# First block of sorted tokens: by matmuls with place matrices, where it was scattered, loaded back and transposed

## The chip, the cores and the metric

One Trainium2 chip, one of its cores. TensorE (PE) multiplies, VectorE (DVE), ScalarE (ACT) and GpSimd (POOL) compute elementwise, SyncE (SP) issues most transfers. The metric is the time of one execution on the device in microseconds, the median over runs.

## The reference, cut to what matters

The network is one diffusion block followed by a second block that ends in a mixture of experts. Only that last part is touched. With 512 tokens of 1024 features it computes

```python
group_p, group_idx = lax.top_k(jax.nn.softmax(group_logits, axis=-1), 1)     # 1 of 4 groups
exp_p, exp_idx = lax.top_k(jax.nn.softmax(in_group, axis=-1), 2)             # 2 of its 4 experts
h = silu(einsum("td,edf->tef", t, w_gate)) * einsum("td,edf->tef", t, w_up)  # 16 experts, 256 wide
y = einsum("tef,efd->td", h * combine[:, :, None], w_down)
out = layer_norm(ALPHA * t + y, ln2_g, ln2_b)
```

where t itself is a layer norm of the rows that come before (`(x - mean) * rs * g + b`), and `combine` holds the gates of the two chosen experts.

## The kernel before, in words

All engines run hand-written instruction streams that meet at semaphores. Two stages matter.

**Rows and routing (`OutRows`, `Grouping`).** The last dense product leaves the rows before their layer norm in `X`, token-major, four tiles of 128 tokens. DVE takes the logits, picks each token's group and experts, and counts (with a few small PE matmuls, `pe_count`) which place each token gets when tokens are sorted by group. Places 0 to 127 are block 0, the first 128 tokens of group 0; there are `NBLK` = 7 blocks of 128 places. The place of each token is in `D1` (float) and `dest` (integer). The layer norm is made in two passes per tile into `tok`: `dve_rows_first` (subtract the mean, times the gain; line 2939) and `dve_rows_second` (times the reciprocal deviation, plus the bias; line 2946). After each second pass POOL scatters that tile's rows by `dest` to an array `xs` in device memory (line 3017).

**Experts (`moe`).** 28 steps x, four experts for each block b. A step takes three weight slots of 1 MB, called A and B (the up product) and D (down), in the order A0 B0 A1 B1 D0 A2 B2 D1 and so on, 84 in all. SP loads slot s into one of six raw buffers (line 3206) once DVE is done with slot s-6. ACT makes its high part (`hi`, line 3312), DVE the low part (`lo`, line 3376), and PE multiplies three times (high-high, low-high, high-low; lines 3259 to 3261 and 3285 to 3287). Between the products PE turns the hidden rows (`turn_hidden`, line 3269) after DVE's `gate` (line 3393), and ACT and DVE split them again (lines 3333, 3398). The tokens of a block are loaded back from `xs` into `XB` (block 0 at line 3188), turned by eight PE transposes into banks 6 and 7 (`turn_block`, line 3243), and split by ACT (`x_hi`, line 3319) and DVE (`x_lo`, line 3382) into `xsh` and `xsl`. After its last step DVE evacuates and normalises a block (lines 3408 to 3433), and POOL delivers it (line 3224).

Before block 0 starts, SP, ACT (for slot 5) and DVE wait for all four scatters (`scattered`). DVE's order is then: `lo` of slots 0, 1, 2, `x_lo(0)`, `lo` of slots 3, 4, 5, `gate(0)`, `lo` of slot 6, `hidden_lo(0)`. ACT makes the high parts of slots 0 to 3 early; that of slot 4 overwrites `X` and that of slot 5 overwrites `tok`.

Of the kernel before, what the change touches and what calls it, by code (L numbers as in the profile page):

```python
# [8 lines left out]
ALU = mybir.AluOpType  # L9
# [3 lines left out]
P = 128  # L13
D = 1024
KT = D // P
# [8 lines left out]
NCH = T // P  # L24
# [11 lines left out]
RING_RAW, RING_W = 6, 6  # L36
# [8 lines left out]
TMP = CONST + 4608  # L45
MAIN = TMP + 5 * W * 4 + 1024
# [2668 lines left out]
class OutRows:  # L2715
# [218 lines left out]
    def dve_rows_first(self, dve, tok, ts):  # L2934

        nc = self.e.nc
        dve.wait_ge(self.ln_in, 16)
        for t in ts:
            nc.vector.scalar_tensor_tensor(tok[:, t, 0:D], self.X[:, t, :], self.mv[:, t, 0:1], self.LN1[:, 0:D],
                                           ALU.subtract, ALU.mult).then_inc(self.half_row, 1)  # L2940

    def dve_rows_second(self, dve, tok):

        for t in range(NCH):
            dve.wait_ge(self.half_row, t + 1)
            self.e.nc.vector.scalar_tensor_tensor(tok[:, t, 0:D], tok[:, t, 0:D], self.rs[:, t:t + 1],
                                                  self.LN1[:, D:2 * D], ALU.mult, ALU.add).then_inc(self.row_ready, 1)


class Grouping:  # L2950


    def __init__(self, e, late, tok, dest, gsel):
        self.e, self.st, self.late = e, Stage(e, "route"), late
        self.tok, self.dest, self.gsel = tok, dest, gsel
        off = [TMP + 4096]

        def small(n, *dims):
            t = self.st.sb(n, [P] + list(dims), off[0])
            off[0] += (int(np.prod(dims)) * 4 + 31) // 32 * 32  # L2960
            return t

        self.PRI, self.BASE0 = small("pri", 4), small("base0", 4)
        self.LG, self.EX, self.M1, self.EQ, self.MG, self.IN, self.TM, self.MA, self.MB, self.M2, self.ED, self.SM, \
            self.GP, self.W1, self.W2, self.CI = (small(n, NCH, c) for n, c in (
                ("lg", 32), ("ex", 4), ("m1", 1), ("eq", 4), ("mg", 4), ("in", 4), ("tm", 4), ("ma", 4), ("mb", 4),
                ("m2", 1), ("ed", 1), ("sm", 1), ("gp", 1), ("w1", 1), ("w2", 1), ("ci", 4)))
        self.TRI = self.st.sb("tri", [P, P], MAIN + 140032)
        self.PM, self.GT, self.IG = small("pm", NCH, 4), small("gt", NCH, 4), small("ig", NCH, 4 * EPG)
        self.D1 = small("d1", NCH, 1)  # L2970
        self.NT, self.X1, self.X2, self.EE, self.EB, self.C0, self.DB = (
            small(n, 1, 4) for n in ("nt", "x1", "x2", "ee", "eb", "c0", "db"))
        self.LE, self.GB = small("le", 3, 3), small("gb", 3, 1)
        assert off[0] <= TMP + 8192
        self.const_in, self.e1_pre, self.e1_ready, self.e2_pre, self.e2_ready, self.mg_ready, self.count_psum, \
            self.dest_ready, self.rec_ready, self.gsel_ready, self.chain = (
                self.st.sem(n) for n in ("const_in", "e1_pre", "e1_ready", "e2_pre", "e2_ready", "mg_ready", "count_psum",
                                         "dest_ready", "rec_ready", "gsel_ready", "chain"))
        self.late_chain = self.st.sem("late_chain")

    def sp(self, sp):
        d = self.e.dram
        sp.dma_start(self.PRI[:, :], d["priority"]).then_inc(self.const_in, 16)
        sp.dma_start(self.BASE0[:, :], d["group_base"]).then_inc(self.const_in, 16)
        sp.dma_start(self.TRI[:, :], d["before"]).then_inc(self.const_in, 16)
        sp.dma_start(self.tok[:, :, D:REC], d["rec_tail"]).then_inc(self.const_in, 16)

    def pe_count(self, pe):

        nc, e = self.e.nc, self.e  # L2990
        pe.wait_ge(self.mg_ready, 1)
        pe.wait_ge(self.const_in, 64)
        mg = self.MG[:, :, :].rearrange("p t g -> p (t g)")
        nc.tensor.matmul(e.bank[4][:, 0:16], self.TRI[:, :], mg, start=True, stop=False)
        for t in range(NCH - 1):
            nc.tensor.matmul(e.bank[4][:, 4 * t + 4:16], e.ones[:, :],
                             self.MG[:, t, :].unsqueeze(1).to_broadcast([P, NCH - 1 - t, 4]),
                             start=False, stop=t == NCH - 2)
        nc.tensor.matmul(e.bank[5][:, 0:16], e.ones[:, :], mg, start=True, stop=True).then_inc(self.count_psum, 1)

    def act_logits(self, act):
        nc = self.e.nc
# [17 lines left out]
    def dve(self, dve):  # L3020
        e, nc = self.e, self.e.nc
        done = [0]
        V = nc.vector
# [27 lines left out]
                V.tensor_tensor(out[:, :, :], EQ[:, :, :], wide(M2[:, :, :]), ALU.is_equal).then_inc(last_sem, 1)  # L3051
                dve.wait_ge(last_sem, 1)

        dve.wait_ge(self.const_in, 64)
        V.tensor_scalar(self.C0[:, 0, :], self.BASE0[:, :], -1.0, 384.0, ALU.mult, ALU.add)
        V.memset(self.EB[:, :, :], 0.0)
        self.late.dve_logits(dve, LG, self.tok)
# [32 lines left out]
        link(V.tensor_tensor(self.PM[:, :, :], self.PM[:, :, :], MG[:, :, :], ALU.mult))  # L3090
        link(V.tensor_reduce(self.D1[:, :, :], self.PM[:, :, :], AX, ALU.add))
        V.tensor_copy(self.dest[:, :], self.D1[:, :, 0]).then_inc(self.dest_ready, 1)

        dve.wait_ge(self.e1_ready, 1)
        link(V.tensor_reduce(GP[:, :, :], EX[:, :, :], AX, ALU.add))
# [26 lines left out]
def moe(e, lead, late):  # L3122
# [6 lines left out]
    nc = e.nc  # L3129
    st = Stage(e, "moe")  # L3130
    I32, U32 = mybir.dt.int32, mybir.dt.uint32
    tok = st.sb("tok", [P, NCH, REC], MAIN + 81920)
# [19 lines left out]
    route = Grouping(e, late, tok, dest, gsel)  # L3152
# [14 lines left out]
    slot = {key: s for s, key in enumerate(order)}  # L3167
# [6 lines left out]
    with block_of(e) as block:  # L3174
# [58 lines left out]
        def _(pe):  # L3233
# [3 lines left out]

            def turn_block(b):
                pe.wait_ge(xb_in[b % 2], 16 * (b // 2) + 16)
                if b:  # L3240
                    pe.wait_ge(xs_ready, b)
                for k in range(KT):
                    last = nc.tensor.transpose(e.bank[6 + k // 4][:, (k % 4) * P:(k % 4 + 1) * P],
                                               XB[b % 2][:, k * P:(k + 1) * P], e.ident[:, :])
                last.then_inc(x_turn, 1)
# [41 lines left out]
                        last = nc.tensor.matmul(out, c, w[:, cc], start=False, stop=j == EPG - 1 and k == 1)  # L3287
                last.then_inc(pe_slot, 1)

            turn_block(0)  # L3290
            for x in range(NSTEP):
                if x % EPG == EPG - 1 and x // EPG + 1 < NBLK:
                    turn_block(x // EPG + 1)
# [10 lines left out]
        def _(act):  # L3304
# [9 lines left out]
            def x_hi(b):  # L3314
                act.wait_ge(x_turn, b + 1)
                if b >= 2:
                    act.wait_ge(pe_slot, slot["B", EPG * (b - 1) - 1] + 1)
                for n in range(2):
                    last = nc.scalar.activation(xsh[b % 2][:, 4 * n:4 * n + 4, :],
                                                e.bank[6 + n][:, :].rearrange("p (k t) -> p k t", t=P), ACT.Copy)  # L3320
                last.then_inc(xh_done, 1)
# [20 lines left out]
            for s in range(4):  # L3342
                hi(s)
                if s == 1:
                    route.act_second(act)
            act.wait_ge(late.row_ready, NCH)
            hi(4)
            x_hi(0)
            act.wait_ge(scattered, 16 * NCH)
            hi(5)  # L3350
            for x in range(NSTEP + 1):
# [17 lines left out]
        def _(dve):  # L3369
# [4 lines left out]
            def lo(s):  # L3374
                dve.wait_ge(hi_done, s + 1)
                nc.vector.tensor_tensor(wl[s % RING_W][:, :], raw[s % RING_RAW][:, :], wh[s % RING_W][:, :].bitcast(F32),  # L3376
                                        ALU.subtract).then_inc(lo_done, 1)

            def x_lo(b):
                dve.wait_ge(xh_done, b + 1)  # L3380
                for n in range(2):
                    last = nc.vector.tensor_tensor(xsl[b % 2][:, 4 * n:4 * n + 4, :],  # L3382
                                                   e.bank[6 + n][:, :].rearrange("p (k t) -> p k t", t=P),
                                                   xsh[b % 2][:, 4 * n:4 * n + 4, :].bitcast(F32), ALU.subtract)
                last.then_inc(xs_ready, 1)
# [48 lines left out]
                                               ).then_inc(y_done, 1)  # L3434

            route.dve_groups(dve)
            dve.wait_ge(scattered, 16 * NCH)
            for n in range(3):
                lo(n)
            x_lo(0)  # L3440
            for n in range(3, RING_W):
                lo(n)
            for x in range(NSTEP + 1):
                if x % EPG == EPG - 1 and x // EPG + 1 < NBLK:
# [63 lines left out]
def layout_inputs(i):  # L3508

    g = {n: np.asarray(v) for n, v in i.items()}  # L3510
    dram = {}
# [4 lines left out]
    xf, q, k, v, o, gt, gf, gm = np.split(w_in, np.cumsum([512, 1024, 1024, 1024, 1024, 16, 1024]), axis=1)  # L3516
# [60 lines left out]
    dram["ln2_rows"] = np.ascontiguousarray(np.broadcast_to(np.concatenate([g["ln2_g_2"][0], g["ln2_b_2"][0]]), (P, 2 * D)))  # L3577
    dram["ln1_rows"] = np.ascontiguousarray(np.broadcast_to(np.concatenate([g["ln1_g_2"][0], g["ln1_b_2"][0]]), (P, 2 * D)))
    dram["group_base"] = np.ascontiguousarray(np.broadcast_to(P * np.arange(4, dtype=np.float32), (P, 4)))
    dram["before"] = np.triu(np.ones((P, P), np.float32), 1)  # L3580
    dram["sgu_ln"] = np.ascontiguousarray(
        np.broadcast_to(np.concatenate([g["sgu_ln_g_2"][0], g["sgu_ln_b_2"][0]]), (P, 2 * D)))
# [19 lines left out]
    s, t = np.meshgrid(np.arange(P), np.arange(P), indexing="ij")  # L3602
# [3 lines left out]
    tok, ch = np.kron(dft(T // 64), dft(64)), dft(P)  # L3606
    tok = tok.reshape(T, T // GRID, GRID)[:, :, 0:FQ].reshape(T, FH)
# [160 lines left out]
```

## Time and profile before

| | us |
|---|---|
| median of 3 runs | 2806.11 (2799.13, 2806.11, 2806.12) |
| the profiled execution, its own time | 2809.66 |
| its span in the trace | 2807.4 |
| mean granted TensorE clock over the span | 0.961 |

All times of the trace are counted from the start of the span. The clock is given as a share of 2.4 GHz, so 0.50 is 1.2 GHz. PE is busy for 93% of the span, DVE for 42%; the expert stage begins near 2538 us and fills the last tenth of the span.

### The profile page before, as it was taken

How to read it: one execution, taken by the hardware profiler on the slowest of the kernel's cores; microseconds unless marked ns; L12 is line 12 of the kernel's file. 1: busy time of each engine (PE TensorE's matmuls, PEld its weight loads, DVE VectorE, ACT ScalarE, POOL GpSimd, SP SyncE). 2: the span in 40 equal slices, each digit the busy share in tenths (PEclk: the TensorE clock that was granted, in tenths of full speed). 3: DMA queues.
4: the chain of work that ended last, by engine and by line, in shares of the span. 5: the costliest groups of instructions: out<-in, count | busy, mean ns of one | idle time of the engine just before them, and what ended most of it. 6: DMA issues, size and time to landing. Idle time of an engine off the chain costs nothing. (4 is left out here: it accounts for less than half of the span.)

```text
span 2807.4 us, 35910 instructions
## 1 busy us (share of the span) xinstructions
PE 2620.0 (93%) x14338; PEld 2225.5 (79%) x14338; DVE 1173.0 (42%) x1683; ACT 715.2 (25%) x1151; POOL 1354.3 (48%) x431
## 2 busy tenths in 40 slices
PE   6999999995999899998999997999989999978997
PEld 4888888883889788875788885778987898877775
DVE  5112011226476454126311225355425135348997
ACT  5111000102220432101210103344431011126775
POOL 0443465451564045675577775465436776710000
PEclk8999999997999999999999998899999999978999
DMA  7443212123322013232123224120012232429994
GB/s 288 180 189 138 71 60 73 43 65 118 116 75 75 4 42 112 83 127 90 60 86 103 102 83 181 60 76 16 1 61 76 92 131 91 179 107 368 375 381 179
DMA packets 52445, 334.02 MB, mean 119 GB/s; under 512 B 6516, under 2 KB 7540, under 8 KB 19616
## 3 DMA queue, kind: packets, MB, share of 16 engines
q1 hardware_dynamic: 50736, 326.49, 31.6%
q0 software_dynamic: 1584, 5.78, 0.5%
q8 instruction: 88, 1.44, 0.2%
q14 instruction: 37, 0.30, 0.0%
HBM read 313.89 MB, written 22.07 MB: 120 GB/s over the span
## 5 line engine op out<-in xcount | busy, mean ns | idle before, releaser
L186 POOL TENSOR_TENSOR whi<-raw,one_col 128x2048 fp32r<-128x2048 f32 (+2 forms) x158 | 526.3, 3331 | 891.1 <-PE bank L206 790.4
L189 POOL TENSOR_TENSOR wlo<-raw,whi 128x2048 fp32r<-128x2048 f32 (+2 forms) x158 | 698.2, 4419 | 12.4
L204 PE MATMUL bank<-uh_a,whi 128*128 128x512 f32 (+1 forms) x704 | 239.3, 340 | 1.6 <-DVE ul_a L499 1.6
L205 PE MATMUL bank<-ul_a,whi 128*128 128x512 f32 (+1 forms) x704 | 237.6, 338 | 0.0
L206 PE MATMUL bank<-uh_a,wlo 128*128 128x512 f32 (+1 forms) x704 | 237.3, 337 | 0.0
L3376 DVE TENSOR_TENSOR moe_wl<-moe_raw,moe_wh 128x2048 fp32r<-128x2048 f32 x84 | 189.4, 2282 | 7.2 <-DMA xs_scratch<-moe_tok,moe_dest 5.4
L3312 ACT ACTIVATE moe_wh<-moe_raw 128x2048 fp32r<-128x2048 f32 x84 | 159.8, 1912 | 25.6 <-PE bank L3287 19.6
L204 PEld LDWEIGHTS bank<-uh_a,whi 128*128 128x128 f32 x704 | 134.2, 191 | 21.4 <-issue 3.7
L206 PEld LDWEIGHTS bank<-uh_a,wlo 128*128 128x128 f32 x704 | 134.1, 190 | 14.3
L204 PE MATMUL bank<-uh_b,whi 128*128 128x512 f32 x352 | 138.3, 393 | 7.5 <-DVE ul_b L682 6.5
L205 PEld LDWEIGHTS bank<-ul_a,whi 128*128 128x128 f32 x704 | 134.2, 191 | 13.7
L205 PE MATMUL bank<-ul_b,whi 128*128 128x512 f32 x352 | 137.9, 392 | 0.0
L206 PE MATMUL bank<-uh_b,wlo 128*128 128x512 f32 x352 | 137.9, 392 | 0.0
L3224 POOL DMA_INDIRECT out_dram<-moe_y,moe_rows x7 | 6.7, 952 | 264.3 <-DVE moe_y L3433 264.3
L204 PE MATMUL bank<-fa_hh,whi 128*128 128x512 f32 (+1 forms) x352 | 118.7, 337 | 1.0 <-DVE fa_hl L822 1.0
L205 PE MATMUL bank<-fa_hl,whi 128*128 128x512 f32 (+1 forms) x352 | 118.4, 336 | 0.0
L206 PE MATMUL bank<-fa_hh,wlo 128*128 128x512 f32 (+1 forms) x352 | 118.3, 336 | 0.0
L785 ACT ACTIVATE fa_sil<-bank 128x512 f32<-128x512 f32 x22 | 13.2, 599 | 402.6 <-PE bank L206 402.6
L204 PE MATMUL bank<-xh_r,whi 128*128 128x512 f32 x256 | 101.8, 398 | 5.5 <-POOL wlo L189 3.3
L206 PE MATMUL bank<-xh_r,wlo 128*128 128x512 f32 x256 | 100.7, 393 | 0.0
L205 PE MATMUL bank<-xl_r,whi 128*128 128x512 f32 x256 | 100.6, 393 | 0.0
L3259 PE MATMUL bank<-moe_wh,moe_xsh 128*128 128x512 f32 x224 | 91.2, 407 | 2.8 <-DVE moe_xsl L3382 2.8
(545 smaller groups left out, 6398.7 us busy)
## 6 DMA issues: line engine op xcount, KB each, us to landing
moe_raw<-moe_w_dram SPq DMA_DIRECT2D x84, 1024.0 KB, 7.4
cond_ring<-w_ada_dram SPq DMA_DIRECT2D x27, 1024.0 KB, 6.9
raw<-gu_a_dram SPq DMA_DIRECT2D x22, 1024.0 KB, 5.1
raw<-gu_b_dram SPq DMA_DIRECT2D x22, 1024.0 KB, 4.9
raw<-wqkv_dram SPq DMA_DIRECT2D x12, 1024.0 KB, 4.8
raw<-dn_a_dram SPq DMA_DIRECT2D x16, 704.0 KB, 4.1
raw<-dn_b_dram SPq DMA_DIRECT2D x16, 704.0 KB, 4.1
n_ada<-w_ada_dram SPq DMA_DIRECT2D x9, 1024.0 KB, 19.5
```

The costliest lines, as they stand in the source:

```text
L186: e.nc.gpsimd.tensor_tensor(e.whi[p][:, 0:f], e.raw[p][:, 0:f], e.one_col[:, 0:1].to_broadcast([P, f]), ALU.mult).then_inc(e.w_hi, 1)
L189: e.nc.gpsimd.tensor_tensor(e.wlo[p][:, 0:f], e.raw[p][:, 0:f], e.whi[p][:, 0:f].bitcast(F32), ALU.subtract).then_inc(e.w_split, 1)
L204: e.nc.tensor.matmul(out, wh, xh, start=first, stop=False)
L205: e.nc.tensor.matmul(out, wh, xl, start=False, stop=False)
L206: return e.nc.tensor.matmul(out, wl, xh, start=False, stop=last)
L785: last = nc.scalar.activation(sil[p][:, 0:T], e.bank[2 * p][:, :], ACT.Silu)
L3224: nc.gpsimd.indirect_dma_start(out=e.dram["out"], out_offset=bass.IndirectOffsetOnAxis(ap=rows[r][:, :], axis=0), in_=Y[r][:, :], in_offse ...
L3259: nc.tensor.matmul(out, xsh[b % 2][:, k, :], w[:, cc], start=k == 0, stop=False)
L3312: nc.scalar.activation(wh[s % RING_W][:, :], raw[s % RING_RAW][:, :], ACT.Copy).then_inc(hi_done, 1)
L3376: nc.vector.tensor_tensor(wl[s % RING_W][:, :], raw[s % RING_RAW][:, :], wh[s % RING_W][:, :].bitcast(F32), ALU.subtract).then_inc(lo_done, 1)
```

## The change

Block 0 no longer waits for scatter, load and transposes. DVE makes a place matrix `HOT` for each of the four token tiles: in the row of a token it has the token's reciprocal deviation in the column of its place, where that is below 128, and zero elsewhere. PE multiplies the half-normed rows (mean taken off, times the gain) by it, four tiles accumulated, and adds the bias with a matmul that contracts over one partition. What comes out is block 0's tokens, turned, in banks 6 and 7. For that the first pass of the layer norm writes to `X` and not to `tok`. The scatter and the load of `XB` for block 0 stay, since the gates and the residual are read from there. ACT's `x_hi(0)` moves ahead of `hi(4)`; DVE's order becomes `lo(0)`, `x_lo(0)`, `lo(1)`, the wait for the scatters, and `lo` of slots 2 to 5. One more constant of 64 KB is loaded.

```diff
 def dve_rows_first
-            nc.vector.scalar_tensor_tensor(tok[:, t, 0:D], self.X[:, t, :], self.mv[:, t, 0:1], self.LN1[:, 0:D],
+            nc.vector.scalar_tensor_tensor(self.X[:, t, :], self.X[:, t, :], self.mv[:, t, 0:1], self.LN1[:, 0:D],
 def dve_rows_second
-            self.e.nc.vector.scalar_tensor_tensor(tok[:, t, 0:D], tok[:, t, 0:D], self.rs[:, t:t + 1],
+            self.e.nc.vector.scalar_tensor_tensor(tok[:, t, 0:D], self.X[:, t, :], self.rs[:, t:t + 1],
 Grouping.sp
+        sp.dma_start(self.SLOT[:, :], d["slot_row"]).then_inc(self.const_in, 16)
...
+    def pe_first_block(self, pe, turned):
+
+        nc, e, late = self.e.nc, self.e, self.late
+        pe.wait_ge(late.half_row, NCH)
+        pe.wait_ge(self.hot_ready, 1)
+        for k in range(KT):
+            out, cols = e.bank[6 + k // 4][:, (k % 4) * P:(k % 4 + 1) * P], slice(k * P, (k + 1) * P)
+            for t in range(NCH):
+                nc.tensor.matmul(out, late.X[:, t, cols], self.HOT[:, t, :], start=t == 0, stop=False)
+            last = nc.tensor.matmul(out, late.LN1[0:1, D + k * P:D + (k + 1) * P], e.ones[0:1, :], start=False, stop=True)
+        last.then_inc(turned, 1)
...
         V.tensor_copy(self.dest[:, :], self.D1[:, :, 0]).then_inc(self.dest_ready, 1)
+        for t in range(NCH):
+            last = V.tensor_scalar(self.HOT[:, t, :], self.SLOT[:, :], self.D1[:, t, :], self.late.rs[:, t:t + 1],
+                                   ALU.is_equal, ALU.mult)
+        last.then_inc(self.hot_ready, 1)
 moe, PE
-            turn_block(0)
+            route.pe_first_block(pe, x_turn)
 moe, ACT
+            x_hi(0)
             act.wait_ge(late.row_ready, NCH)
             hi(4)
-            x_hi(0)
             act.wait_ge(scattered, 16 * NCH)
             hi(5)
 moe, DVE
             route.dve_groups(dve)
+            lo(0)
+            x_lo(0)
+            lo(1)
             dve.wait_ge(scattered, 16 * NCH)
-            for n in range(3):
-                lo(n)
-            x_lo(0)
-            for n in range(3, RING_W):
+            for n in range(2, RING_W):
                 lo(n)
```

## Rows read from the trace of the kernel before

**Rows 1.** Busy time by engine, clock and DMA share, three stretches.

```profile
core 0: us, PE busy (x) PEld busy (x) DVE busy (x) ACT busy (x) POOL busy (x), PEclk, DMA share, GB/s
...
2517.00:2538.00 21.00, 2.03 (x9) 1.66 (x9) 15.18 (x26) 5.44 (x5) 5.12 (x4) 0.50 0.55 206
...
2546.00:2580.00 34.00, 34.00 (x159) 28.03 (x158) 30.84 (x22) 27.77 (x24) 0.00 (x0) 1.00 0.97 396
2580.00:2620.00 40.00, 39.08 (x181) 31.89 (x180) 39.76 (x37) 31.61 (x28) 0.95 (x1) 1.00 0.96 364
```

**Rows 2.** Timeline of PE around the start of block 0.

```profile
2533.18 1.97 PE L3243 MATMUL bank<-ident,moe_xb 128*128 128x128 f32 x8 [19.93 <-DMA moe_xb<-xs_scratch]
2537.94 0.76 PE L3259 MATMUL bank<-moe_wh,moe_xsh 128*128 128x512 f32 x1 [2.79 <-DVE moe_xsl L3382]
```

**Rows 3.** Timeline of DVE: start, duration, work, idle time before.

```profile
2517.59 0.17 DVE L3092 CAST moe_dest<-route_d 128x4 uint32<-128x4 f32 x1
...
2518.78 4.87 DVE L2946 SCALAR_TENSOR_TENSOR moe_tok<-moe_tok,late_rs,LN 128x1024 f32<-128x1024 f32 x4
...
2524.29 0.17 DVE L3119 CAST moe_gsel<-route_gb 128x3 int32<-128x3 f32 x1
2529.90 6.70 DVE L3376 TENSOR_TENSOR moe_wl<-moe_raw,moe_wh 128x2048 fp32r<-128x2048 f32 x3 [5.44 <-DMA xs_scratch<-moe_tok,moe_dest]
2536.51 1.28 DVE L3382 TENSOR_TENSOR moe_xsl<-bank,moe_xsh 128x512 fp32r<-128x512 f32 x2
2537.71 6.68 DVE L3376 TENSOR_TENSOR moe_wl<-moe_raw,moe_wh 128x2048 fp32r<-128x2048 f32 x3
2546.16 0.48 DVE L3393 SCALAR_TENSOR_TENSOR moe_h<-moe_sil,moe_xb,bank 128x256 f32<-128x256 f32 x1 [1.76 <-ACT moe_sil L3327]
2547.96 2.29 DVE L3376 TENSOR_TENSOR moe_wl<-moe_raw,moe_wh 128x2048 fp32r<-128x2048 f32 x1 [1.32 <-ACT moe_wh L3312]
...
2565.59 1.29 DVE L3382 TENSOR_TENSOR moe_xsl<-bank,moe_xsh 128x512 fp32r<-128x512 f32 x2 [0.66 <-ACT moe_xsh L3319]
```

**Rows 4.** The same for DVE, the last idle time before it is full.

```profile
2575.30 0.42 DVE L3398 TENSOR_TENSOR moe_hl<-bank,moe_hh 128x256 fp32r<-128x256 f32 x1 [1.02 <-ACT moe_hh L3333]
```

**Rows 5.** Timeline of DVE, a tensor-scalar of the size of a place matrix.

```profile
2128.50 0.68 DVE L1661 TENSOR_SCALAR VTD<-VTD,RS 128x128 f32<-128x128 f32 x3
```

**Rows 6.** Timeline of PE, float32 work with 128 columns at either clock.

```profile
1906.67 1.52 PE L2114 MATMUL bank<-ident,proj_vs 128*128 128x128 f32 x8 [2.81 <-DVE VTD L2438]
...
1908.85 2.91 PE L2184 MATMUL bank<-delta_xt,delta_lm 128*128 128x128 f32 x16
...
2341.46 1.95 PE L2683 MATMUL bank<-WS,VT 128*128 128x128 f32 x16
```

**Rows 7.** Clock in two stretches after PE resumed at 2537.94.

```profile
2540.00:2542.00 2.00, 2.00 (x6) 1.52 (x6) 2.00 (x1) 0.00 (x0) 0.00 (x0) 0.50 1.04 437
2542.00:2544.00 2.00, 2.00 (x10) 1.60 (x9) 2.00 (x2) 0.00 (x0) 0.00 (x0) 0.92 1.05 438
```

**Rows 8.** Timeline of ACT: the split of block 0, and slot 12.

```profile
2535.18 1.09 ACT L3319 ACTIVATE moe_xsh<-bank 128x512 fp32r<-128x512 f32 x2 [9.60 <-PE bank L3243]
...
2560.16 1.91 ACT L3312 ACTIVATE moe_wh<-moe_raw 128x2048 fp32r<-128x2048 f32 x1
```

**Rows 9.** Timeline of POOL, the second and third scatter.

```profile
2522.59 1.90 POOL L3017 DMA_INDIRECT xs_scratch<-moe_tok,moe_dest  x1 [0.30 <-DVE moe_tok L2946]
2524.79 0.95 POOL L3017 DMA_INDIRECT xs_scratch<-moe_tok,moe_dest  x1 [0.30 <-issue]
```

**Rows 10.** Timeline of PE, the first turn of hidden rows.

```profile
2548.27 0.38 PE L3269 MATMUL bank<-ident,moe_h 128*128 128x128 f32 x2
```

**Rows 11.** Timeline of SP, the loads of block 0, slots 6 and 7, slots from 12.

```profile
2529.89 0.33 SPq L3188 DMA_DIRECT2D moe_xb<-xs_scratch  x1
2532.22 2.53 SPq L3206 DMA_DIRECT2D moe_raw<-moe_w_dram  x2
...
2550.65 23.99 SPq L3206 DMA_DIRECT2D moe_raw<-moe_w_dram  x10
```

**Rows 12.** DMA issues of the page: KB each, median us to landing.

```profile
moe_raw<-moe_w_dram SPq DMA_DIRECT2D x84, 1024.0 KB, 7.4
```

**Rows 13.** Costliest groups of the page: the deliveries; busy us, mean ns.

```profile
L3224 POOL DMA_INDIRECT out_dram<-moe_y,moe_rows x7 | 6.7, 952 | 264.3 <-DVE moe_y L3433 264.3
```

More of the change, by code:

```diff
@@ L2974, in __init__ @@
         assert off[0] <= TMP + 8192
+        self.SLOT, self.HOT = self.st.sb("slot", [P, P], MAIN + 140544), self.st.sb("hot", [P, NCH, P], TMP + 2048)
+        self.hot_ready = self.st.sem("hot_ready")
         self.const_in, self.e1_pre, self.e1_ready, self.e2_pre, self.e2_ready, self.mg_ready, self.count_psum, \
@@ L2991, in pe_count @@
         pe.wait_ge(self.mg_ready, 1)
-        pe.wait_ge(self.const_in, 64)
+        pe.wait_ge(self.const_in, 80)
         mg = self.MG[:, :, :].rearrange("p t g -> p (t g)")
@@ L3052, in first_max @@
                 dve.wait_ge(last_sem, 1)
-        dve.wait_ge(self.const_in, 64)
+        dve.wait_ge(self.const_in, 80)
         V.tensor_scalar(self.C0[:, 0, :], self.BASE0[:, :], -1.0, 384.0, ALU.mult, ALU.add)
@@ L3239, in turn_block @@
                 pe.wait_ge(xb_in[b % 2], 16 * (b // 2) + 16)
-                if b:
-                    pe.wait_ge(xs_ready, b)
+                pe.wait_ge(xs_ready, b)
                 for k in range(KT):
@@ L3579, in layout_inputs @@
     dram["group_base"] = np.ascontiguousarray(np.broadcast_to(P * np.arange(4, dtype=np.float32), (P, 4)))
+    dram["slot_row"] = np.ascontiguousarray(np.broadcast_to(np.arange(P, dtype=np.float32), (P, P)))
     dram["before"] = np.triu(np.ones((P, P), np.float32), 1)
```

## Prediction

> **What bounds the kernel now.** I read the busy time by stretches first, then the timelines of PE, DVE, ACT, POOL and SP between 2510 and 2610 us, where all of the change lies, and last the later stretches, to see whether a shift there reaches the end.
>
> From 2517 to 2538 PE is busy for 2.03 of 21 us [rows 1]: this is the hole that the change is about. PE's wait ends with the load of block 0 from `xs` (19.93 us idle), and after eight transposes it waits 2.79 us more for `x_lo(0)` [rows 2]. DVE is free at 2524.46, idles 5.44 us until the scatters have landed, makes `lo` of slots 0 to 2, `x_lo(0)`, and `lo` of slots 3 to 5, and is through at 2544.39 [rows 3]. So before the change the first product, at 2537.94, is set by DVE's queue (three `lo` ahead of `x_lo(0)`), and that queue by the scatter. The transposes end at 2535.15, 1.4 us before DVE comes to them.
>
> Then two engines share the pace. From 2546 to 2580 PE is full (34.00 of 34 us) and DVE has 3.2 us to spare; from 2580 on DVE is full (39.76 of 40 us) and PE nearly so [rows 1]; the three stretches of 40 us behind it read the same within 0.1 us for DVE. Nothing after that has slack that an earlier start would merely fill. DVE's last idle time before it is full is at 2575.30 and ends on ACT's part of the hidden rows, thus on PE [rows 4]. Hence the rule for this change: the end moves by as much as PE moves in block 0, so long as DVE can follow, which has 1.76 + 1.32 + 0.66 + 1.02 us of idle time in block 0 to give up [rows 3, 4].
>
> **Added on DVE before the block.** Four tensor-scalars of 128x128. Three such take 0.68 us, 0.28 us the last and 0.20 each before it [rows 5], so four take 0.88. They stand behind the cast that starts at 2517.59, at about 2517.67 [rows 3], and end at 2518.55. Bounds: 0.88 if that row holds, 4 x 0.34 = 1.4 us by an estimate from `gate`, which takes 0.48 us for 256 columns; 128 columns fewer at the 1.1 ns per column of `lo` (2.28 us for 2048) make 0.34 [rows 3]. I take the first, the same operation at the same size. Behind them wait the second pass (its four rows start 0.9 later and end at 2524.5) and `dve_groups`, to 2525.3, and so POOL's scatters, by 0.9 as well. Everything else of the row stage is the same work: the first pass writes to another tile, the second reads from it. The 64 KB constant is one more small load far ahead of its use. I take both at nothing; the cover of the constant is the last dense product.
>
> **Added on PE.** 8 x (4 + 1) = 40 float32 matmuls of 128 columns. In the trace a float32 matmul is two instructions (line 2683 is called 8 times for the 16 shown), a transpose one. So eight instructions become eighty. At the full clock 16 take 1.95 us, that is 0.112 apart with 0.27 for the last; at half clock 8 take 1.97 us, 0.213 apart with 0.47 for the last [rows 2, 6]. The block would take 79 x 0.112 + 0.27 = 9.1 us at 2.4 GHz and 79 x 0.213 + 0.47 = 17.3 us at 1.2 GHz. PE has been idle since 2513 and the clock is at 0.50 in this stretch [rows 1], so it starts slow. How long? When PE resumed at 2537.94 the clock was at 0.50 up to 2542 and averaged 0.92 over the next 2 us, so it rose at 2542.3, after 4.4 us [rows 7]. In the dense float32 stream that began at 1906.67, the 16 instructions from 1908.85 on took 2.91 us, 0.96 more than the 1.95 of full clock; at 0.101 us each that makes some 9.5 slow ones, and the rise lies near 1910.9, 4.2 us after the stream began [rows 6]. I take 4.4 us: 20.6 instructions in it, 59.4 x 0.112 = 6.7 behind it, 0.2 for the end, 11.3 us in all. From 2518.6 that ends at 2529.9.
>
> **The path to the first product.** `x_hi(0)` takes 1.09 us [rows 8]: 2531.0. DVE made `lo(0)` meanwhile (2525.3 to 2527.5) and waits. `x_lo(0)` takes 1.2 us [rows 3]: 2532.3, and PE can start at 2532.4, 5.5 us before the 2537.94 of now. What is late next is DVE: `gate(0)` stands behind `lo` of slots 1 to 5. At 2.21 us each (6.62 for three from 2529.90 to 2536.51, [rows 3]) that is 11.05 us, so 2543.3; `gate(0)` adds 0.45 and the first turn of hidden rows starts at 2543.8. Now it is at 2548.27 [rows 10]. PE meanwhile has 36 matmuls to do. At full clock 34 us hold 159 instructions [rows 1], 0.21 each, 7.7 us; should the clock be low again for 4.4 us after the gap, that adds half of it, 2.2 us, and PE is through at 2542.3. So the clock of these products is not on the path. The gain at this point is 4.5 us. From here PE runs through as now; DVE stands 2.9 us ahead of now at `gate(0)` (2543.75 against 2546.64) and can give up the idle times counted above, 3.0 us behind it, so it can follow 4.5.
>
> **What moves with it.** ACT's `hi(4)` goes behind `x_hi(0)` and `hi(5)` behind that: 2531.0 + 2 x 1.91 = 2534.8, needed by DVE at 2541.1, hidden. The wait for the scatters stands behind `lo(1)` at 2534.5. They landed at 2529.9 [rows 11]; 0.9 later is 2530.8, so 3.7 us of cover. `lo(0)` now runs while POOL writes the third and fourth scatter. In the trace a scatter beside DVE's row pass took 1.90 us and one beside an idle DVE 0.95 [rows 9]; taken at 1.90 for both, the landing is 2532.7, still hidden. SP issues slot 6 behind the scatter wait, 1.3 us before the 2532.22 of now at best, and slot 7 after `lo(1)`, as now [rows 11]. The load of `XB`, issued at 2530.8 and some 7 us under way, is needed by `gate(0)` at 2543.3.
>
> The Trainium skill speaks against the new place of `lo(0)`: SBUF — State Buffer, section "SBUF: two separate sides", says that a VectorE operation with two SBUF inputs and a GpSimd operation that reads SBUF hold the shared port pair as an exclusive lock, the other waiting for the whole instruction. By that a scatter would wait for up to one `lo`. The 1.90 beside the 0.95 agrees in direction; the seven deliveries of finished blocks, all but the last beside a full DVE, average 0.95 each and do not show it [rows 13]. Neither reaches the 3.7 us of cover: one `lo` is 2.3 us.
>
> **Sum.** 2809.66 is the profiled execution's own time, 2.3 us more than its span, and 3.55 above the median of the runs. The span goes from 2807.4 to 2802.9, and the median from 2806.11 to 2801.6.
>
> **Rivals.**
>
> *The weight loads keep the old pace (chance 0.15).* The transfers are at 0.97 of the engines' time, 396 GB/s, where PE would have to run ahead [rows 1], and the refill starts only 1.3 us earlier. Against it: slot 12, issued at 2550.65, is used at 2560.16 [rows 8, 11], 9.5 us later, while a load takes 7.4 [rows 12], and so there are 2 us in hand at the tightest place that I found. If it held, the gain is the 1.3 us of the refill: 2804.8.
>
> *The clock stays low through the block (0.08), the case on the other side.* The block then takes 17.3 us, to 2535.9; `x_hi(0)` 2537.05, `x_lo(0)` 2538.3, five `lo` and `gate(0)` 2549.8, against 2548.27 of now: 1.5 us slower, 2807.6. It decides from a block of 15.8 us on, which is a clock that rises after the 66th of the 80 instructions. For it: the row at 2517 to 2538 shows half clock, and the stage before has stretches in which narrow matmuls let it fall. Against it: the float32 stream of 128 columns at 1908.85 raised it.
>
> *No low clock at all, or a short one (0.10).* The block at 9.1 us ends 2.2 us sooner: a gain of 6.7 us, 2799.4, if the loads keep up.
>
> *The change does nothing (0.05).* If the hole were filled but DVE, full from 2580 on, had no idle time to give up. The four idle times speak against it. 2806.1.
>
> **How the numbers follow.** Forecast, a gain of 3 to 6 us: 0.62. The three runs before differ by 7 us among themselves, so less than 0.3% (8.4 us) can't be told from no change here, and every case lies inside that bound. Only the spread of runs can carry it over: the lower of them less 4.5 is 2794.6, which would be 0.4% under the median. Faster by over 0.3%: 0.12; within: 0.84; slower: 0.04. Range: 2795 (the lower level with the forecast's gain) to 2808 (low clock throughout). The forecast's own range is 2800 to 2803.
>
> **What would show it.** Right: PE's line of the block starts near 2518.6 with 80 instructions and lasts 10 to 12 us; the first product near 2532.4; a new wait of PE for `gate(0)` of about 1.5 us; first turn of hidden rows near 2543.8; DVE's idle times between 2544 and 2580 shrunk from 4.8 us to some 1 to 2; the end of the span 4.5 us earlier. Wrong: half clock through the whole block; ACT's `hi` waiting for a landing (none does now); the scatter landing later than `lo(1)`; or a changed pace after 2580.

## Result, and the profile after

The change makes the kernel slower: 2808.84 us median over 12 runs against 2801.71 for the kernel before over 12 runs on the same chips, a ratio of 1.0022 with a 95% interval of 1.0013 to 1.0031, that is +6.2 us (+3.6 to +8.7); the ratio is taken over all these runs, the two medians alone differ by 7.1 us. Forecast was a gain of 4.5 us. The forecast time of 2801.6 us that went with it counts for nothing by itself: it started from 2806.11, the median of three runs, and over 12 runs the kernel before is at 2801.71 without any change.

Two traces cannot be compared by their spans here. The cast to `dest`, the last step of the routing and common to both, starts at 2517.59 us in the first trace of before and at 2511.77 in that of after; a second trace of the kernel before (below) has it at 2506.68. What lies ahead of the cast differs by 10.9 us between two executions of one program. What lies behind repeats within 0.1 us in these two, so all times below are counted from the start of the cast, as differences of the starts that the timelines give.

| us from the cast | before | before again | after |
|---|---|---|---|
| block 0 in PE starts | 15.6 | 15.6 | 1.3 |
| block 0 in PE ends | 17.6 | 17.5 | 23.2 |
| `x_lo(0)` starts | 18.9 | 18.9 | 24.4 |
| first product starts | 20.4 | 20.4 | 25.8 |
| first turn of hidden rows | 30.7 | 30.6 | 37.1 |
| evacuation of block 0 starts | 62.9 | 62.8 | 69.3 |
| end of span | 289.8 | 289.7 | 296.5 |

So the loss is 6.7 us in the traces, in line with the 6.2 of the runs; 6.4 of it stand at the first turn of hidden rows and stay to the end. PE's timeline of after, against [rows 2]:

```profile
2513.10 2.05 PE L3012 MATMUL bank<-route_hot,X 128*128 128x128 f32 x8 [5.66 <-DVE route_hot L3109]
2515.08 0.79 PE L3013 MATMUL bank<-ones,LN 1*128 1x128 f32 x2
2515.80 2.08 PE L3012 MATMUL bank<-route_hot,X 128*128 128x128 f32 x8
...
2532.16 2.08 PE L3012 MATMUL bank<-route_hot,X 128*128 128x128 f32 x8
2534.17 0.79 PE L3013 MATMUL bank<-ones,LN 1*128 1x128 f32 x2
2537.55 0.76 PE L3277 MATMUL bank<-moe_wh,moe_xsh 128*128 128x512 f32 x1 [2.59 <-DVE moe_xsl L3400]
```

Two things can be seen. Eight instructions over 128 partitions, which at half clock would be followed by the next after 8 x 0.213 = 1.70 us, are followed after 1.98; and the two of the bias, over one partition (`1*128`), take 0.72 where two of the others take 0.43. A group of ten lasts 2.7 us instead of 2.13. The clock, against [rows 1]:

```profile
core 0: us, PE busy (x) PEld busy (x) DVE busy (x) ACT busy (x) POOL busy (x), PEclk, DMA share, GB/s
2513.00:2524.00 11.00, 10.90 (x41) 9.13 (x41) 8.59 (x17) 0.00 (x0) 6.86 (x4) 0.50 0.31 125
2524.00:2535.00 11.00, 10.96 (x41) 9.10 (x40) 0.00 (x0) 0.00 (x1) 0.00 (x0) 0.50 0.55 211
...
2546.00:2580.00 34.00, 33.80 (x157) 27.68 (x156) 32.36 (x24) 27.80 (x24) 0.00 (x0) 1.00 1.01 422
2580.00:2620.00 40.00, 39.08 (x182) 31.86 (x181) 39.78 (x37) 31.49 (x29) 0.95 (x1) 1.00 0.98 390
```

PE is busy without a gap for 22 us, and its clock stays at 1.2 GHz all that time. Behind 2580 the pace is that of before. DVE, against [rows 3]:

```profile
2511.77 0.17 DVE L3107 CAST moe_dest<-route_d 128x4 uint32<-128x4 f32 x1
2511.85 1.11 DVE L3109 TENSOR_SCALAR route_hot<-route_slot,route_d,late_rs 128x128 f32<-128x128 f32 x4
...
2519.59 2.29 DVE L3394 TENSOR_TENSOR moe_wl<-moe_raw,moe_wh 128x2048 fp32r<-128x2048 f32 x1
2536.12 1.29 DVE L3400 TENSOR_TENSOR moe_xsl<-bank,moe_xsh 128x512 fp32r<-128x512 f32 x2 [14.25 <-ACT moe_xsh L3337]
2537.32 11.09 DVE L3394 TENSOR_TENSOR moe_wl<-moe_raw,moe_wh 128x2048 fp32r<-128x2048 f32 x5
2548.33 0.47 DVE L3411 SCALAR_TENSOR_TENSOR moe_h<-moe_sil,moe_xb,bank 128x256 f32<-128x256 f32 x1
```

DVE idles 14.25 us for the block with one `lo` done, and then has five `lo` before `gate(0)`. POOL's timeline, against [rows 9]:

```profile
2520.01 2.69 POOL L3032 DMA_INDIRECT xs_scratch<-moe_tok,moe_dest  x1 [0.30 <-issue]
2523.00 0.95 POOL L3032 DMA_INDIRECT xs_scratch<-moe_tok,moe_dest  x1 [0.30 <-issue]
```

SP's, against [rows 11]:

```profile
2526.56 0.33 SPq L3207 DMA_DIRECT2D moe_xb<-xs_scratch  x1
2526.93 13.03 SPq L3225 DMA_DIRECT2D moe_raw<-moe_w_dram  x2
```

The third scatter, beside `lo(0)`, takes 2.69 us; the scatters are through at 14.8 from the cast instead of 12.3, still ahead of everything that waits for them. The two loads spread over 13.03 us are slots 6 and 7: the second waits for `lo(1)`.

### The profile page after: what moved, and what is told of

It is laid out like the page before. It is cut to its first block and busy times, and to the rows that moved or that the text cites. A ratio compares the mean times of both kernels' runs of the same rounds, so it can differ in the third digit from the quotient of the medians.

```text
span 2808.3 us, 36061 instructions
## 1 busy us (share of the span) xinstructions
PE 2635.1 (94%) x14410; PEld 2237.7 (80%) x14410; DVE 1173.6 (42%) x1687; ACT 715.3 (25%) x1151; POOL 1356.8 (48%) x431
## 5 line engine op out<-in xcount | busy, mean ns | idle before, releaser
L206 PEld LDWEIGHTS bank<-uh_a,wlo 128*128 128x128 f32 x704 | 133.9, 190 | 14.2
L785 ACT ACTIVATE fa_sil<-bank 128x512 f32<-128x512 f32 x22 | 13.2, 599 | 402.6 <-PE bank L206 402.6
```

What stands on the lines that cost most here:

```text
L206: return e.nc.tensor.matmul(out, wl, xh, start=False, stop=last)
```

## Experiments

Line numbers and names are those of the changed kernel. Four questions: what makes the block long, what of it is the clock, what the new orders cost, and whether a better version is in reach.

**The bias over 128 partitions (e1_full_bias).** The bias rows are equal in all partitions, so times the identity they give the same sum.

```diff
-            last = nc.tensor.matmul(out, late.LN1[0:1, D + k * P:D + (k + 1) * P], e.ones[0:1, :], start=False, stop=True)
+            last = nc.tensor.matmul(out, late.LN1[:, D + k * P:D + (k + 1) * P], e.ident[:, :], start=False, stop=True)
```

> The changed kernel, but the bias of block 0 is added by a matmul that contracts over all 128 partitions (the bias rows, which are equal in all partitions, times the identity) in place of one partition. Same sums, same 80 instructions. Theory A (the one-partition matmuls break the pipeline of PE and with their low activity keep its clock at 1.2 GHz): all 80 instructions 0.213 us apart while slow, a clock that rises after some 4.4 us, the block in 11 to 12 us instead of 21.9, first turn of hidden rows some 31.5 us after the start of the cast to dest instead of 37.1 (before: 30.7), and the run 5 to 6 us faster than the changed kernel, so about level with or up to 2 us faster than the kernel before. Theory B (only the breaks in the pipeline come from them; the clock stays low because of the nearly empty place matrices or of something else): 17.3 us at half clock, turn of hidden rows at 32.5 to 33, about 4.5 us faster than the changed kernel. Theory C (they have nothing to do with it): 21.9 us and no change.

Theory A came out. PE's timeline:

```profile
2508.22 2.04 PE L3012 MATMUL bank<-route_hot,X 128*128 128x128 f32 x8 [5.66 <-DVE route_hot L3109]
2510.05 0.63 PE L3013 MATMUL bank<-ident,LN 128*128 128x128 f32 x2
...
2514.53 1.06 PE L3012 MATMUL bank<-route_hot,X 128*128 128x128 f32 x8
2515.42 0.39 PE L3013 MATMUL bank<-ident,LN 128*128 128x128 f32 x2
...
2534.17 0.44 PE L3287 MATMUL bank<-ident,moe_h 128*128 128x128 f32 x2 [2.86 <-DVE moe_h L3411]
```

The group of ten takes 1.12 us from 2514.53 on, the block 12.1 us instead of 21.9. First turn at 27.3 (before 30.6 to 30.7, after 37.1), evacuation 61.1, end 288.4. Ratio to before 0.9985 (0.9976 to 0.9995), -4.2 us with an interval of -6.7 to -1.4; the traces give -1.3 to -1.4, its edge. One line turns the loss into a small gain. Part of the lead was not kept: it is 3.4 us at the turn and 1.7 at the evacuation. The weight loads did not take it, since ACT waited only 0.4 us for them in this stretch. PE waited 2.86 us for `gate(0)`, and behind that gap the clock fell:

```profile
2531.00:2533.00 2.00, 0.31 (x2) 0.00 (x0) 2.00 (x2) 1.63 (x1) 0.00 (x0) 1.00 1.02 428
2533.00:2535.00 2.00, 0.83 (x4) 0.72 (x5) 2.00 (x3) 0.63 (x2) 0.00 (x0) 0.94 1.01 426
2535.00:2537.00 2.00, 2.00 (x6) 1.61 (x5) 2.00 (x3) 1.90 (x2) 0.00 (x0) 0.50 1.02 430
2537.00:2539.00 2.00, 2.00 (x7) 1.57 (x7) 2.00 (x2) 0.05 (x2) 0.00 (x0) 0.71 1.01 426
```

These averages make 3.4 us at half clock, which cost 1.7 us of full-clock work, as much as was lost.

**No bias (e2_no_bias).** The eight bias matmuls are left out. 

```diff
-                nc.tensor.matmul(out, late.X[:, t, cols], self.HOT[:, t, :], start=t == 0, stop=False)
-            last = nc.tensor.matmul(out, late.LN1[0:1, D + k * P:D + (k + 1) * P], e.ones[0:1, :], start=False, stop=True)
+                last = nc.tensor.matmul(out, late.X[:, t, cols], self.HOT[:, t, :], start=t == 0, stop=t == NCH - 1)
```

> The changed kernel with the eight bias matmuls of block 0 left out (so block 0 lacks the bias in what its experts see). 64 instructions. Theory A: no breaks, clock up after some 4.4 us, 20.6 slow ones and 43.4 fast ones, 9.5 us for the block. Theory B: 64 x 0.213 + 0.3 = 13.9 us at half clock all through.

```profile
2508.14 10.31 PE L3012 MATMUL bank<-route_hot,X 128*128 128x128 f32 x64 [5.66 <-DVE route_hot L3108]
```

10.3 us: theory A again. By 0.213 and 0.112 per instruction some 29 of the 64 were slow, so the clock rose about 6 us after the start. The turn comes at 25.5 and the end at 286.8.

**Fuller place matrices (e3_dense_places).** `ALU.is_equal` becomes `ALU.is_ge`.

```diff
-                                   ALU.is_equal, ALU.mult)
+                                   ALU.is_ge, ALU.mult)
```

> The changed kernel with place matrices that are half full: the comparison is greater-or-equal instead of equal, so block 0 is computed from sums of rows and not from the rows. The one-partition bias matmuls stay. If nearly empty matrices keep the clock low (theory B in one form), the clock rises within the block and it takes under 17 us. Theory A: the clock stays at 0.50 and the block takes 21.9 us as in the changed kernel.

```profile
2509.00:2519.00 10.00, 10.00 (x39) 8.43 (x39) 8.37 (x15) 0.00 (x0) 6.19 (x4) 0.50 0.27 108
2519.00:2530.00 11.00, 11.00 (x42) 9.21 (x41) 0.00 (x0) 0.00 (x0) 0.67 (x1) 0.50 0.61 237
```

Nothing moved: half clock, the block ends at 23.2, the turn at 37.1. That the matrices are almost empty is not the cause.

**The bias over 64 partitions (e8_bias_64).** As in e1, over the lower half.

```diff
-            last = nc.tensor.matmul(out, late.LN1[0:1, D + k * P:D + (k + 1) * P], e.ones[0:1, :], start=False, stop=True)
+            last = nc.tensor.matmul(out, late.LN1[0:64, D + k * P:D + (k + 1) * P], e.ident[0:64, :], start=False, stop=True)
```

> The changed kernel with the bias matmul over 64 partitions, times the first 64 rows of the identity, so that only places 0 to 63 of block 0 get their bias. Are the breaks a matter of one partition or of any change in the number of partitions between neighbouring matmuls? If of any change: 0.72 us for a bias pair as with one partition, and the block above 14 us. If only of very few partitions: 0.43 us for the pair slow, block about 12 us as with 128. The clock rises in either case if half the rows count as activity enough.

```profile
2514.35 0.79 PE L3013 MATMUL bank<-ident,LN 64*128 64x128 f32 x2
2515.08 2.07 PE L3012 MATMUL bank<-route_hot,X 128*128 128x128 f32 x8
...
2526.98 1.16 PE L3012 MATMUL bank<-route_hot,X 128*128 128x128 f32 x8
2528.07 0.48 PE L3013 MATMUL bank<-ident,LN 64*128 64x128 f32 x2
```

The breaks are those of one partition, 0.73 us for the pair. So they come with 64 partitions as with one. The clock, however, rose this time: 0.50 up to 2520 and 0.82 on average from 2520 to 2524, so near 2521.4, 9 us after the start. The block takes 16.2 us. That is one trace.

**A warm start with the one-partition bias (e6_warm_one_row).**

```diff
 def pe_first_block
+        for n in range(16):
+            nc.tensor.matmul(e.bank[3][:, 0:P], e.ident[:, :], e.ident[:, :], start=True, stop=True)
         pe.wait_ge(late.half_row, NCH)
```

> The changed kernel, one-partition bias kept, with 16 float32 matmuls of the identity by itself added on PE in the idle time ahead of the block (their result goes to a bank that nobody reads). It parts the two costs of the one-partition matmuls. If they only keep the clock from rising, the clock, high when the block starts, stays high: the block then shows the breaks alone, 8 x (8 x 0.112 + 0.2 + 0.6) = about 13.5 us. If their low activity also lets it fall, the clock goes to 0.50 within some us of the start of the block and it takes 17 to 21 us.

```profile
2504.61 6.32 PE L3008 MATMUL bank<-ident 128*128 128x128 f32 x32
2510.76 1.06 PE L3014 MATMUL bank<-route_hot,X 128*128 128x128 f32 x8
2511.75 0.48 PE L3015 MATMUL bank<-ones,LN 1*128 1x128 f32 x2
2512.16 1.16 PE L3014 MATMUL bank<-route_hot,X 128*128 128x128 f32 x8
```

The clock reads 1.00 from 2510 to 2522, and the block takes 12.0 us. So the stream with one-partition matmuls in it did not lower a high clock in these 12 us; it only did not raise a low one in 22. Against the 9.1 us of the same warm start with the 128-partition bias (e7, e12) the breaks alone cost 2.9 us at 2.4 GHz. The turn comes at 27.5 and the end at 288.7: in this one trace the warm start by itself, with the one-partition bias kept, also turns the loss into a lead of some 1 us over the kernel before.

**The order of DVE undone (e4_old_order).** All else as changed, the bias over one partition too.

```diff
             route.dve_groups(dve)
-            lo(0)
-            x_lo(0)
-            lo(1)
             dve.wait_ge(scattered, 16 * NCH)
-            for n in range(2, RING_W):
+            for n in range(3):
+                lo(n)
+            x_lo(0)
+            for n in range(3, RING_W):
                 lo(n)
```

> The changed kernel with DVE's order of the kernel before: wait for the scatters, lo of slots 0 to 2, x_lo(0), lo of slots 3 to 5. PE's block is the same 21.9 us. If the loss comes from DVE's queue (five lo behind x_lo(0), 14 us of idle time ahead of it), then DVE is through with its third lo about 20 us after the cast, waits for the block until some 24.5, and gate(0) is done at 32.7 instead of 36.6: turn of hidden rows 4 us sooner than in the changed kernel, 2 us later than before; time about 4 us under the changed kernel. The scatters land at 13.2 after the cast instead of 14.8, since no lo runs beside them. If only the block's length counts, the turn stays within 1 us of the changed kernel's 37.1.

```profile
2517.51 0.95 POOL L3032 DMA_INDIRECT xs_scratch<-moe_tok,moe_dest  x1 [0.30 <-issue]
```

```profile
2543.13 0.48 DVE L3411 SCALAR_TENSOR_TENSOR moe_h<-moe_sil,moe_xb,bank 128x256 f32<-128x256 f32 x1 [1.63 <-ACT moe_sil L3345]
```

The first fence is POOL's timeline, the third scatter, the second DVE's, `gate(0)`. Scatters at 13.3, as expected, and the third takes 0.95 us without a `lo` beside it. But the turn comes at 36.0, only 1.1 us sooner, since `gate(0)` now waits 1.63 us for PE: DVE's queue and PE's first products, which start at 25.8 in either, are nearly tied. The span ends at 295.3, 1.2 us sooner than in after, and the ratio to before is 1.0015 (1.0005 to 1.0025). The order is not what makes the change slow.

**More of DVE's work ahead of `x_lo(0)` (e5_full_bias_order).** The bias of e1, and:

```diff
-            lo(0)
-            x_lo(0)
-            lo(1)
-            dve.wait_ge(scattered, 16 * NCH)
-            for n in range(2, RING_W):
+            for n in range(3):
+                lo(n)
+            x_lo(0)
+            dve.wait_ge(scattered, 16 * NCH)
+            for n in range(3, RING_W):
                 lo(n)
```

> The kernel with the 128-partition bias (e1_full_bias) and another order of DVE: lo of slots 0, 1, 2, then x_lo(0), then the wait for the scatters and lo of slots 3 to 5. In e1_full_bias PE waited 2.9 us for gate(0) and its clock fell for 3.4 us behind that gap. Theory: DVE's five lo behind x_lo(0) make that gap. With three of them in DVE's idle time, DVE gets to x_lo(0) about 14.5 us after the cast, as ACT is done, and gate(0) ends near 23.3; PE, which starts the first product near 16.0 and needs 8.2 us for 36 matmuls, sets the first turn of hidden rows at 24.3 (27.3 in e1_full_bias, 30.7 before), with no gap and no fall of the clock. Evacuation of block 0 near 57 after the cast (61.1 in e1_full_bias, 62.9 before); time 4 to 5 us under e1_full_bias, 0.3% under before. Rival: the scatters are held up by two more lo beside them (by up to 2 us each) and the weight loads, already at full rate, cannot follow; then ACT or gate(0) wait for transfers, and the gain over e1_full_bias is 0 to 2 us.

The turn came at 24.3 exactly, and the rival took the gain behind it. ACT's waits for loads (total us, number, longest):

```profile
ACT moe_wh L3330 <- DMA moe_raw<-moe_w_dram: 7.1, 8, 2.8
```

Evacuation at 61.6, later than in e1, and the end at 288.9; ratio 0.9992 (0.9983 to 1.0001). With the lead at 6.3 us the weight loads bind: at some 420 GB/s the DMA engines show a share of 1.01 from 2536 on.

**The refill first (e9_early_refill).** On top of e5, SP's wait for the scatters and the load of block 0 go from ahead of slot 6 to ahead of slot 9.

```diff
-                if s == RING_RAW:
+                if s == RING_RAW + 3:
                     sp.wait_ge(scattered, 16 * NCH)
                     sp.dma_start(XB[0][:, :], e.dram["xs"][0:P, :]).then_inc(xb_in[0], 16)
-                if s == RING_RAW + 2:
+                if s == RING_RAW + 4:
```

> e5_full_bias_order, but SP loads weight slots 6, 7 and 8 before it waits for the scatters and loads block 0 back (before, SP waited for the scatters first, although DVE had freed the raw buffers). In e5_full_bias_order PE turned the hidden rows at 24.3 us after the cast as expected, but ACT then waited 7.1 us in eight waits for weight loads and evacuation of block 0 came at 61.6 instead of 57. Theory: the refill, which began with the scatter's landing at 15.9, is what was late; it now begins at 10.2. ACT's waits for loads go to under 2 us, evacuation at 57 to 58.5, the end 3 to 4.5 us sooner than e5_full_bias_order: about 0.25 to 0.3% under before. Rival: the loads are at full rate whatever their start, or they delay the scatters and the load of block 0 so much that gate(0) waits; then evacuation stays at 61 to 62.

The rival again, by DVE's and then ACT's waits:

```profile
DVE moe_wl L3394 <- DMA xs_scratch<-moe_tok,moe_dest: 7.0, 1, 7.0
```

```profile
ACT moe_wh L3330 <- DMA xs_scratch<-moe_tok,moe_dest: 7.9, 1, 7.9
```

Beside three loads of 1 MB the scatters take a median of 7.0 and up to 11.5 us from issue to landing (3.6 to 4.3 before) and are through at 22.7. Turn 29.9, evacuation 62.1, end 289.4, ratio 0.9997 (0.9988 to 1.0007). Both theories of the loads were half right: ACT no longer waits for weights, and DVE waits for scatters.

This trace shows one thing more. PE's stream in the block is that of e1 and e5, yet the clock rose sooner:

```profile
2511.00:2513.00 2.00, 2.00 (x10) 2.00 (x11) 1.86 (x6) 0.00 (x0) 0.00 (x0) 0.50 0.00 0
2513.00:2515.00 2.00, 2.00 (x16) 2.00 (x16) 2.00 (x3) 0.00 (x0) 1.00 (x1) 0.80 0.00 0
```

The block starts at 2510.92 and the rise lies near 2513.8, 2.9 us later; the block takes 10.5 us. In e1 and e5 it was about 6 us later, and 12.1. So the rise of one and the same stream differs by 3 us between executions.

**Warm starts with the full bias (e7, e10, e12).** The 16 matmuls of e6 added, as the edit of e6 has them, to e5, e9 and e1; they write to a bank that nothing reads then.

> e5_full_bias_order with the same 16 matmuls ahead of the block. If PE runs at 2.4 GHz when the block starts, the block takes 9.1 us instead of 12. DVE then comes to x_lo(0) later than ACT is done (14.5 against 12), so the gain over e5_full_bias_order is at most nothing to 0.5 us: DVE's queue is the bound. Time level with e5_full_bias_order within 1 us.

> e9_early_refill with the 16 float32 matmuls of the identity ahead of the block. Block in 9.1 us instead of 12, but DVE's three lo hold x_lo(0) at 14.4 as in the kernel with them and the late refill, where the first turn of hidden rows even came at 26.5 against 24.3, since the clock fell in the longer gap between block and first product. So level with e9_early_refill or up to 1.5 us slower.

> e1_full_bias (changed order of DVE as in the change, bias over 128 partitions) with 16 float32 matmuls of the identity ahead of the block. Block 9.1 us instead of 12.1, x_lo(0) at 11.7 after the cast instead of 14.6, and with five lo behind it the first turn of hidden rows at 24.4 instead of 27.3. PE again waits some 3 us for gate(0) and loses some 1.7 us to the low clock behind that. If the weight loads follow, evacuation of block 0 at 58.2 and the run 2 to 3 us under e1_full_bias; if the loads bind as in e5_full_bias_order, evacuation at 59 to 61 and 0 to 2 us.

The block takes 9.1 to 9.2 us in all three. e7: turn 26.5, evacuation 59.3, end 286.6 from the cast, 0.9993 (0.9982 to 1.0003). e10: 28.9, 61.0, 288.3, 0.9995 (0.9986 to 1.0004). e12: turn 24.4 as expected, evacuation 60.0, end 287.3, 0.9992 (0.9981 to 1.0002); ACT waited 8.1 us for weight loads there. All three end 1.4 to 3.2 us before the kernel before in the traces and can't be told from it, nor from e1, in the runs. My note that e7 had no more than 0.5 us over e5 to win was wrong by its trace (2.4 us sooner at the end), and the runs don't resolve it.

The turn of e7 comes 2.2 us later than that of e5 because its clock fell to 0.50 in the idle time of 5.2 us between block and first product. Such falls can't be foretold from the length of the idle time in these traces. Of six with 2.6 us between block and first product, e2, e8 and e12 have the fall and e1, e5 and e6 have not; 4.0 us (e9) and 5.1 and 5.2 us (e10, e7) have it. In e7, e9, e10 and e12 it came while PE was still idle, in e2 and e8, and behind `gate(0)` in e1, only after it had resumed.

**The kernel before once more (e11_before_again).**

> The kernel before, word for word, for a second trace of it. The traces of all changed kernels reach the cast to dest between 2506.7 and 2511.8 us, that of before at 2517.6, though nothing ahead of the cast differs but 64 KB of constants and where the first pass writes. If that is spread between executions, this trace has its cast anywhere from 2505 to 2518; if the change moved it, at 2517 again. From the cast on it should repeat: turn of hidden rows 30.7, evacuation of block 0 62.9, end 289.8 after it, each within 1 us.

Cast at 2506.68, turn 30.6, evacuation 62.8, end 289.7: spread ahead of the cast, a repeat behind it.

## Why the prediction was wrong

**The step that failed** is the price of PE's block, 80 instructions 0.213 or 0.112 us apart with a clock that rises after 4.4 us, 11.3 us in all. It took 21.9. Two parts, both from the bias matmuls over one partition, told apart by e1, e6 and e12. Breaks: at half clock 79 x 0.213 + 0.47 would be 17.3 us, so 4.6 are the breaks on either side of each bias pair (0.6 us per group of ten). Clock: with the breaks gone it rises about 6.0 us after the start (0.72 on average from 2512 to 2516 in e1) and the block takes 12.1, so 5.2 us are the clock, or 6.8 by the early rise of e9. 4.6 + 5.2 is the 9.8 us by which the turn moved from after to e1. I had taken the price of the bias from rows of full height, and no row of before that I used had a change of height inside a stream. One stood right behind the stream of [rows 6]:

```profile
1911.69 1.15 PE L2139 MATMUL bank<-R,SEL 8*128 8x128 f32 x8
1912.77 0.49 PE L2142 MATMUL bank<-KF 128*128 128x128 f32 x2
```

At full clock eight instructions over 8 partitions are followed by the next after 1.08 us, where eight of full height take 8 x 0.112 = 0.90. A price for the breaks could have been read there, though not what became of the clock.

**The 4.4 us themselves** rest on one sound reading and one wrong one. The float32 stream of [rows 6] was no start at half clock:

```profile
1904.00:1906.00 2.00, 0.00 (x0) 0.00 (x0) 1.93 (x4) 1.25 (x3) 0.00 (x0) 1.00 0.00 0
1906.00:1908.00 2.00, 1.33 (x9) 1.18 (x10) 1.78 (x3) 1.07 (x2) 0.00 (x0) 0.86 0.00 0
1908.00:1910.00 2.00, 2.00 (x11) 2.00 (x11) 1.69 (x4) 0.60 (x1) 0.94 (x1) 0.50 0.00 0
1910.00:1912.00 2.00, 2.00 (x14) 1.88 (x14) 0.01 (x1) 0.80 (x2) 2.00 (x3) 0.78 0.04 8
```

The clock was at 1.00 when PE resumed at 1906.67 after 2.81 us of idle time, fell near 1907.4, and came back near 1910.9. The row does not tell how long a cold stream stays slow. It shows what happened behind `gate(0)` in e1: an idle time of 2.8 us, work resumed at full clock, then 3.4 us at half clock. The trace of before held this warning too.

The Trainium skill has a rule that I should have weighed: TensorEngine Tiling (Array Packing), section "Tiling Modes", says that changing the tiling mode, and not just the tile, drains TensorE; its modes differ in the rows of a tile, 128, 64 or 32. That a matmul over 1 or 64 partitions between full-height ones is such a change is my reading. The breaks of after against e1, and of e6 against e12, agree with it (0.6 us per bias pair at half clock, 0.39 at full).

**The rival** "the clock stays low" happened, at a chance of 0.08 and with too small a price: 17.3 us for the block instead of 21.9, since it lacked the breaks. Its point of decision, a block of 15.8 us, held for the turn and not for the end. e1 (block 12.1) and e8 (16.2) lie on either side: the turn comes 3.3 us sooner and 0.8 later than before, so a straight line puts it level at 15.4 us; the end comes 1.3 sooner and 1.2 later, level at 14.2 us, since e1 loses part of its lead behind the turn.

**The path behind the block** was right in its parts. `x_hi(0)` 1.1 us, `x_lo(0)` 1.2, five `lo` and `gate(0)` 11.5 as stated. With the block at its intended length, e1 has the turn at 27.3 where 26.2 was forecast: 0.3 for place matrices (1.11 us instead of 0.88), 0.8 for the block.

**"From here PE runs through as now"** was wrong. The wait for `gate(0)` that I had named (1.5 us, measured 2.9 in e1, where the products ran at full clock) is followed by 3.4 us at half clock, which cost 1.7 of the 3.4 us of lead. "The clock of these products is not on the path" held with the order of the change: in e1 PE is through with them at 24.4 and `gate(0)` ends at 27.2, and in e12, where they began at half clock, PE is through at 23.0 and `gate(0)` ends at 24.4. I had asked what the clock does to the work ahead of the gap and not to that behind it.

**The weight loads** were given 2 us in hand. In after they didn't bind, since nothing came early; in e5 and e12, with leads of 6.3 us, ACT waited 7 to 8 us for them. The mechanism was rightly named. It takes most of the lead of e5 and part of that of e12; e1 loses its part to the clock, and e9 and e10 wait for scatters. No run settles the chance of 0.15 for a lead of 4.5 us: with 3.4 us (e1) ACT waited 0.4 us for loads, with 4.1 us (e7) 4.9 us.

**The scatters beside `lo(0)`.** Landing was forecast between 13.2 and 15.1 from the cast and came at 14.8. One scatter beside a `lo` took 2.69 and not 1.90 us, 1.74 over the 0.95 of e4, where no `lo` ran beside it. It began at 2520.01, within `lo(0)` (2519.59 to 2521.88), and ended 0.82 us after it, about as if it had begun when `lo(0)` ended. In e5, where `lo(1)` runs beside the fourth scatter, that one takes 1.90 us instead of 0.95 and ends 0.82 us after `lo(1)`. The Trainium skill (SBUF — State Buffer, "SBUF: two separate sides") describes a lock between GpSimd operations and those VectorE operations that have two SBUF inputs, held for a whole instruction; these times agree with it. The deliveries, which I had held against it, are no counter-example:

```profile
2602.97 1.28 DVE L3382 TENSOR_TENSOR moe_xsl<-bank,moe_xsh 128x512 fp32r<-128x512 f32 x2
2603.33 0.95 POOL L3224 DMA_INDIRECT out_dram<-moe_y,moe_rows  x1 [76.33 <-DVE moe_y L3433]
```

The DVE work beside the first five is `x_lo`, which reads a PSUM bank and only one tile in SBUF, and beside the last two DVE is idle. `lo` reads two. The longer scatters cost nothing in after, since nothing waited for them.

**Open.** What in the one-partition stream kept the clock down is shown only as far as: not the contents of the place matrices, not the float32 matmuls of full height, and not a thing that lowers a high clock within 12 us. Three traces (after, e3, e4) stay low for the whole block, four without the short matmuls rise after 2.9 to 6.2 us (e1, e2, e5, e9). Whether 64 partitions really delay the rise is open: 9 us in one trace, where like streams differ by 3. Whether e1's lead in the runs (4.2 us) beyond its trace (1.4) is more than spread is not settled either; a second trace of e1 was not taken.

## To carry to other kernels

Give a small term of an accumulation (a bias) the same number of partitions as its neighbours, for instance equal rows times the identity: one line was worth 9.8 us of a 22 us block here, and 8.1 at the end of the span. When a stall is filled, count the next queue on every engine, and what an idle time of TensorE did to its clock, within it and behind it. Before a row is taken as a start at half clock, read the clock ahead of it. Where the start of a program spreads by more than the change is worth, count times from the last instruction that both versions share.

## What the hardware showed beyond what I expected

- Alternating 128 partitions with 1 or 64 costs 0.6 us per excursion at 1.2 GHz and 0.39 at 2.4, for a pair of 128-column float32 instructions.
- TensorE was busy for 22 us without a gap at 1.2 GHz and the clock did not rise, in three traces. With 64-partition excursions it rose after 9 us (one trace), with none after 2.9 to 6.2 (four traces).
- An idle time of 2.86 us was followed by 3.4 us at half clock that began only after work had resumed. Idle times of 2.6 us were followed by half clock in three traces and not in three others.
- A scatter issued on POOL beside a DVE operation that reads two SBUF tiles ended 0.82 us after that operation: 2.69 us instead of 0.95.
- Scatters of 516 KB each beside 1 MB loads took up to 11.5 us to land instead of some 4.
